# Feed-forward in-products in seven products instead of eight, accumulated over ScalarE's copies between PSUM banks

## The reference

```python
def swiglu(x, w_in, w_out):
    gate, up = jnp.split(x @ w_in, 2, axis=-1)
    return (jax.nn.silu(gate) * up) @ w_out
...
        h = h + 0.5 * swiglu(rms_norm(h, g[0]), P['ffn_w_in'][l, 0], P['ffn_w_out'][l, 0])
```

## Time and profile before

| | |
|---|---|
| Median of 3 runs | 2955.61 us (2951.46 to 2957.7) |
| Profiled execution | 2960.64 us, span 2959.0 us |
| Mean granted TensorE clock | 0.942 of full speed |
| TensorE busy | 2794.9 us, 94% |
| VectorE busy | 1185.8 us, 40% |
| ScalarE busy | 806.5 us, 27% |
| GpSimd busy | 282.6 us, 10% |
| 88 loads of in-weights | 1,024 KB each, 4.8 us to landing |

### The profile page before, as it was taken

The page is one execution under the profiler, slowest core; times in us unless marked ns, Lnnn a source line. Parts: engine busy times, 40 slices in busy tenths (PEclk is TensorE's granted clock), DMA queues, the critical chain, the costliest instruction groups (busy, mean ns, idle before and its releaser), DMA issues. The chain is left out here.

```text
span 2959.0 us, 56832 instructions
## 1 busy us (share of the span) xinstructions
PE 2794.9 (94%) x25177; PEld 2551.7 (86%) x25177; DVE 1185.8 (40%) x1738; ACT 806.5 (27%) x1261; POOL 282.6 (10%) x288
## 2 busy tenths in 40 slices
PE   7999969998999899999998989999998889999997
PEld 7999966776899746999997879999995568999997
DVE  4333355176333251433334123333444443433335
ACT  4212212132222100222221053212226762322221
POOL 1000000001111110000001200000007860000000
PEclk9999989999998557999998999999998997999998
DMA  6222210210000000322224622222222010222222
GB/s 233 82 89 86 77 64 15 71 58 30 4 3 4 33 29 26 131 82 80 95 69 120 162 100 85 85 100 85 71 74 65 23 44 29 88 90 79 99 69 75
DMA packets 36806, 214.84 MB, mean 73 GB/s; under 512 B 5232, under 2 KB 5360, under 8 KB 20880
## 3 DMA queue, kind: packets, MB, share of 16 engines
q1 hardware_dynamic: 27936, 174.34, 17.1%
q0 software_dynamic: 8720, 38.28, 4.4%
HBM read 202.49 MB, written 12.17 MB: 73 GB/s over the span
## 5 line engine op out<-in xcount | busy, mean ns | idle before, releaser
L518 PE MATMUL banks<-xh,wh 128*128 128x272 f32 x3072 | 638.7, 289 | 30.3 <-DVE wl L1484 18.0
L518 PE MATMUL banks<-xh,wl 128*128 128x272 f32 x3072 | 637.5, 289 | 0.0
L518 PE MATMUL banks<-xl,wh 128*128 128x272 f32 x3072 | 635.0, 288 | 0.0
L518 PEld LDWEIGHTS banks<-xh,wh 128*128 128x128 f32 x3072 | 485.5, 189 | 31.1 <-DVE wl L1484 23.4
L518 PEld LDWEIGHTS banks<-xl,wh 128*128 128x128 f32 x3072 | 484.7, 189 | 0.0
L518 PEld LDWEIGHTS banks<-xh,wl 128*128 128x128 f32 x3072 | 481.2, 189 | 0.0
L1484 DVE TENSOR_TENSOR wl<-raw,wh 128x2048 fp32r<-128x2048 f32 (+2 forms) x160 | 323.9, 2024 | 109.8 <-ACT wh L1133 109.7
L1133 ACT ACTIVATE wh<-raw 128x2048 fp32r<-128x2048 f32 (+2 forms) x160 | 270.7, 1692 | 260.5 <-PE banks L518 243.9
L518 PE MATMUL banks<-hh,wl 128*128 128x272 f32 x1408 | 291.4, 288 | 0.0
L518 PE MATMUL banks<-hh,wh 128*128 128x272 f32 x1408 | 291.0, 288 | 0.0
L518 PE MATMUL banks<-hl,wh 128*128 128x272 f32 x1408 | 290.2, 288 | 0.0
(11 more groups left out here) (301 smaller groups left out, 3030.6 us busy)
## 6 DMA issues: line engine op xcount, KB each, us to landing
raw<-in_w_in SPq DMA_DIRECT2D x88, 1024.0 KB, 4.8
raw<-in_w_out SPq DMA_DIRECT2D x32, 768.0 KB, 4.2
raw<-in_w_out SPq DMA_DIRECT2D x32, 640.0 KB, 3.9
raw<-in_w_rk SPq DMA_DIRECT2D x8, 1024.0 KB, 4.8
arena<-in_pages_c POOLq DMA_DIRECT2D x32, 256.0 KB, 7.6
raw<-in_w_kv SPq DMA_DIRECT2D x6, 1024.0 KB, 4.8
raw<-in_w_v SPq DMA_DIRECT2D x4, 1024.0 KB, 4.8
raw<-in_w_o SPq DMA_DIRECT2D x4, 1024.0 KB, 4.8
```

Of the source, the lines that this page charges most:

```text
L518: ins = mm(pst[:, bank + half, 0:HALF], wt[:, s, w], a[:, half * HALF:(half + 1) * HALF], start=first, stop=last)
```

## The change

An in-slot is seen as a 2 x 2 by 2 x 2 product of blocks: gate and up on one side, even and odd input tiles in the middle, the two token halves on the other side. Seven products of blocks take the place of eight (Strassen's scheme in Winograd's form). For this:

- **Weights** come in seven pieces of 512 columns: three straight from the raw slot, four sums. GpSimd makes two of them (`weight_sums`), VectorE two (in `weights`). ScalarE makes each high part, VectorE each low part, into one ring of seven pieces, which the slot in work frees piece by piece. Before, it was one instruction of 2,048 columns on each engine; now it is nine of 512 on VectorE and seven on ScalarE.
- **Activations** come in four groups j of seven operands (three blocks and four sums of 272 columns). ScalarE scales two tiles into a staging place, GpSimd makes the four sums in a chain (`operand_sums`), ScalarE the high parts (3 and then 4 operands), VectorE the low ones (`low_operands`).
- **Products** of 12 matmuls each go into one bank: 0 to x, 1 to w, 2 to x, 3 to y, 4 to x, 5 to w, 6 to z. ScalarE copies x to y after product 0, w to `sg` after 1, x to w after 2, x to z after 4 (`snap`), and TensorE accumulates on the copies. The first slot of a block (`fresh`) goes through groups as they come, and has six opening matmuls. VectorE makes up from `sg` and the banks by two additions of 272 columns, scales the gate, multiplies, and splits the hidden tile (`tail`) one slot later.
- **Stages** are 6, 6, 6 and 4 hidden tiles (`FT_IN`), so there are eight stages in a block, and there are 128 out-slots where there were 64, with 36, 36, 36 and 24 matmuls. The first two out-slots are interleaved by hidden tile.
- **GpSimd's loads** (LoRA, `g2`, `expand`, `cw1`, the table `att`) are moved behind its sums.
- Squares and root have another buffer (`rr` takes the root), and `operands_of` and `first_weights` stand at the ends of `wo`, `bo` and the out-stages.

```diff
-FTA = 12
-FTB = FT - FTA
+FT_IN = (6, 6, 6, 4)
...
+            def eighth(bank, quarter, f, b, js, start, stop):
+
+                for j in js:
+                    w = slice((4 * quarter + j) * P, (4 * quarter + j + 1) * P)
+                    xh_j, xl_j = xop_h[f][j][:, b, :], xop_l[f][j][:, b, :]
+                    for wt, x, first, last in ((ring_h, xh_j, start and j == 0, False), (ring_h, xl_j, False, False),
+                                               (ring_l, xh_j, False, stop and j == 3)):
+                        ins = mm(pst[:, bank, 0:HALF], wt[:, w], x, start=first, stop=last, skip_group_check=True)
+                return ins
...
+                else:
+                    eighth(x_bank, 0, f, 0, range(4), True, True).then_inc(eighth_done, 1)
+                    part(1)
+                    eighth(w_bank, 1, f, 5, range(4), True, True).then_inc(eighth_done, 1)
+                    part(2)
+                    snapped(1)
+                    eighth(x_bank, 2, f, 4, range(4), False, True).then_inc(eighth_done, 1)
+                    part(3)
+                    eighth(y_bank, 3, f, 1, range(4), False, True).then_inc(eighth_done, 1)
+                    part(4)
+                    snapped(3)
+                    eighth(x_bank, 4, f, 3, range(4), False, True).then_inc(eighth_done, 1)
+                pe.wait_ge(w_split[s], i + (ks + 1))
+                eighth(w_bank, 5, f, 6, range(4), False, True).then_inc(eighth_done, 1)
+                part(6)
+                snapped(4)
+                eighth(z_bank, 6, f, 2, range(4), False, True).then_inc(multiplied[s], 1)
...
+                for s in range(2):
+                    take_split(s, k0, ks)
+                    for ft in range(tiles - 2):
+                        tile(s, ft)
+                pe.wait_ge(hid_done[0], hidden + tiles // 2)
+                for s in range(2):
+                    tile(s, tiles - 2)
+                pe.wait_ge(hid_done[1], hidden + tiles // 2)
+                for s in range(2):
+                    tile(s, tiles - 1).then_inc(multiplied[s], 1)
+                with pe.Fori(1, pairs) as i:
...
```

ScalarE's order in a slot:

```diff
+                    act.wait_ge(eighth_done, 6 * k + 1)
+                    act.activation(y, x, ACT.Copy).then_inc(snap, 1)
+                    following(0)
...
+                    act.wait_ge(eighth_done, 6 * k + 2)
+                    act.activation(sg[:, s, 0:HALF], w, ACT.Copy).then_inc(snap, 1)
+                    following(1)
+                    act.wait_ge(eighth_done, 6 * k + 3)
+                    act.wait_ge(snap, 4 * k + 2)
+                    act.activation(w, x, ACT.Copy).then_inc(snap, 1)
+                    if t == 0 and n is not None:
+                        norm(n, 4)
+                    if t:
+                        tail(t - 1)
+                    following(2)
+                    act.wait_ge(eighth_done, 6 * k + 4)
+                    following(3)
+                    act.wait_ge(eighth_done, 6 * k + 5)
+                    act.activation(z, x, ACT.Copy).then_inc(snap, 1)
+                    following(4)
+                    act.wait_ge(eighth_done, 6 * k + 6)
+                    following(5)
+                    act.wait_ge(multiplied[s], k0 + t // 2 + 1)
+                    following(6)
+                    act.wait_ge(taken[s], k0 + t // 2 + 1)
+                    act.activation(sg[:, s, :], sg[:, s, :], ACT.Silu).then_inc(gate_done[s], 1)
```

VectorE's order in a slot (`following(e)` is piece e of the next slot's weights):

```diff
+                    following(0)
+                    following(1)
+                    if t:
+                        tail(t - 1)
+                    if t == 0 and before:
+                        before()
+                    following(2)
+                    following(3)
+                    dve.wait_ge(snap, 4 * k + 4)
+                    dve.tensor_tensor(up[1], x, sg[:, s, 0:HALF], ALU.add).then_inc(up_done, 1)
+                    following(4)
+                    dve.wait_ge(eighth_done, 6 * k + 6)
+                    dve.tensor_tensor(up[0], w, sg[:, s, 0:HALF], ALU.add).then_inc(up_done, 1)
+                    following(5)
...
+                    following(6)
```

GpSimd's sums, and their order in front of block 0:

```diff
+                    pool.wait_ge(landed[s], 16 * (k0 + t // 2 + 1))
+                    if n:
+                        pool.wait_ge(part_split, 6 * n - 4)
+                    pool.tensor_tensor(s3, raw_part(s, 0, 0), raw_part(s, 1, 0), ALU.subtract).then_inc(pool_sums, 1)
+                    if n:
+                        pool.wait_ge(part_split, 6 * n - 1)
+                    pool.tensor_tensor(s1, raw_part(s, 1, 0), raw_part(s, 1, 1), ALU.add).then_inc(pool_sums, 1)
...
-            for s in range(2):
-                pool.wait_ge(landed[s], 16 * 2)
+            for j in range(4):
+                operand_sums(0, j)
+            weight_sums("inA0")
```

More of the change, by code:

```diff
@@ L1133, in split, with pipeline, pair @@
                 act.activation(wh[:, s, 0:cols], raw[:, s, 0:cols], ACT.Copy).then_inc(w_hi[s], 1)
-            def pipeline(name, finish, following, first=None, unroll=False):
+            def pipeline(name, finish, following=None, after=None, begun=False, unroll=False):
                 pairs = STAGES[name][1]
[L1139 to L1142, removed]
+                def pair(i, begun=False):
+                    if not begun:
+                        split(name, i, 1)
                     finish(i, 0)
@@ L1183, in norm @@
                 act.wait_ge(sum_done, n + 1)
-                act.activation(halves(sg[:, 0, :]), bank2(bank), ACT.Sqrt, bias=eps[:, 0:1], scale=1.0 / D)\
+                act.activation(halves(rr[:]), bank2(bank), ACT.Sqrt, bias=eps[:, 0:1], scale=1.0 / D)\
                    .then_inc(root_done, 1)
-            def ffn(f, n, following=None, before=None, scaled=None):
[L1189 to L1204, removed]
@@ new lines, in ffn @@
+            def ffn(f, n, following=None, before=None, scaled=None):
+                for x, c in enumerate("ABCD"):
+                    out, k = f"out{c}{f}", end_of(f"out{c}{f}")
+                    in_stage(f"in{c}{f}", out, before if c == "A" else None)
+                    if c == "D":
+                        pipeline(out, squares(out, n, scaled), following, begun=True, unroll=scaled is not None)
+                    else:
+                        nxt = f"in{'ABCD'[x + 1]}{f}"
+                        pipeline(out, lambda i, s: None, *first_weights(nxt, k), begun=True)
@@ L1218, in _ @@
             act.wait_ge(eps_set, 3)
-            for ft in range(DT):
[L1220 to L1227, removed]
+            for j in range(4):
+                act.wait_ge(x_in[j], 16)
+                operands(0, Q_G00, j)
+                if j == 1:
+                    weights("inA0", 0, 0)
+                if j:
+                    operand_sums(0, j - 1)
+            operand_sums(0, 3)
+            for e in range(1, 7):
+                weights("inA0", 0, e)
+            for ft in range(DT):
+                square(0, ft, ft % 2)
             act.wait_ge(const_in, 16)
@@ L1574, in add @@
+            def add(name, tiles, factor, n=None, scaled=None, rooted=None, operands=None):
                 k0 = STAGES[name][0]
```

479 lines of the change are left out of this document (371 added, 108 removed).

## The result

The changed kernel takes 3,035.2 us (median of 4; 3,021.0 to 3,054.1) where the kernel before took 2,956.7 in the same series: ratio 1.0266, 95% interval 1.0223 to 1.0309. It is slower by 79 us. The forecast was 12 us more, and its range ended at 3,012. The profiled execution is the fastest of the four: 3,020.96 us, span 3,019.3, mean granted clock 0.930 (0.942 before).

What follows compares the result with a forecast made beforehand. TensorE, busy 94% of the span, was taken to bound the kernel. Terms -132.3 + 3.5 + 33 + 56 + 52 = +12 gave 2,973 profiled, forecast median 2,968 us (+0.4%), range 2,928 to 3,012.

Steps and rivals of the forecast that it cites:

- Waits and stages B to D: In-slots: 3.5 us lost to semaphore waits of seven products, plus 33 us as VectorE's loop outlasts TensorE's in later in-stages.
- Stages A: First in-stage of each block: late operands and weights delay the first scaling, 56 us lost in all (50 to 75).
- Out-stages, with `q`: Third out-slot waits for a weight buffer, stage D's cycle outlasts its matmuls, `q`'s first split is late: 52 us (44 to 60).
- the steady loop: In-slots of stages B to D: GpSimd's sums hold VectorE, so the scaling comes every 10.9 us against TensorE's 10.53.
- Rival 1: GpSimd's hold of VectorE is short, 0.8 us; TensorE sets the loop; -21 us, 2,935; chance 0.32.
- rival 2: GpSimd's hold of VectorE is long, 1.45 us; loop 11.6 us; +71 us, 3,027; chance 0.10.
- rival 3: The clock falls to 1.2 GHz in the 16 new out-stage holes; 26 us more, 2,994; chance 0.16.
- the operand sum of GpSimd at 0.65 us: Stage A: each of four chained GpSimd sums of 272 columns takes 0.65 us before the first weight pieces and copy.
- the term of block 2: Stage A, f=2: GpSimd's stores and 12 us of operand sums precede slot 0's end, near 1793.6; loss 16 us.
- Then six pieces and eight squares, 36, before the first copy: Stage A of block 0: ScalarE's operands, pieces and squares delay its first copy to 36 us; scaling at 50, loss 18.
- have tens of microseconds before use and are costed at nothing: Moved GpSimd loads (LoRA, `cw1`, table of distances): an out-stage of 24 us covers 12 us of the longest; cost nothing.
- D's cycle: Out-stage D: VectorE's cycle of 3.5 us against 3.01 of matmuls, five times; with the hole 5.5 us a layer.

## Why the prediction was wrong

The sum was to be +12 in the profiled execution; the blocks gave +85.4. Removing 132.3 is right, so 217.7 us were added, not 144.5. Two terms of the sum were too small, the stages A and the out-stages, and the fall of the clock was in neither. By stage (length less the slots' matmuls at 0.1253, and less what the kernel before loses there; how the slow matmuls divide is good to 3 us):

| Term | said | measured | of it slow matmuls |
|---|---|---|---|
| Waits and stages B to D | 36.5 | 37 | 0 |
| Stages A | 56 | 95 | 12 |
| Out-stages, with `q` | 52 | 86 | 21 |

**Right.** The mechanism of the steady loop and its size: period 10.95 (10.9), first scaling 13.9 (13.3), six slots in 66.5 us (66.4). GpSimd's sum takes 1.27 to 1.30 us undisturbed, more than the 1.18 that I took, and yet its hold in these slots is 1.0 to 1.1 as assumed: VectorE's operation began 0.2 us or more after it, so that two errors cancel, which was luck. The estimate from the Trainium skill ("GPSIMD Engine Reference", section 3.1) was 1.12; the trace has 1.27, and it decides. ScalarE's copy between banks took 0.38, not 0.43. The holes were 2.06 (1.9) in A to C and 3.24 (3.0) in D. Rival 1 fell with the duration, rival 2 with the period.

**Wrong, first: the clock (33 us).** The sum put it at nothing. It was rival 3 with 16 x 1.6 = 26 us at a chance of 0.16, set aside since "the holes are a quarter as long". I compared with the only fall that the rows showed, after 7.1 us, and took the length as evidence where the rows bounded nothing below it. In the runs a hole of 2.06 us was enough in 41 of 80 cases; of those up to 1.96 us, which the steady loop leaves, one did it. The stages A, with several waits of 2 to 13 us each, weren't in that rival at all.

**Wrong, second: stage A (27 us at full clock).** The step that failed is the operand sum of GpSimd at 0.65 us: it took 0.75 to 0.77 alone and up to 1.8 beside VectorE's low parts, which the prediction priced for weight sums and not here. The 16 sums of a block took 18.7 us in blocks 0 and 2, where 16 at 0.65 are 10.4 and the term of block 2 had 12; the chain of four in block 1 took 4.4 us, not 2.6. By block the stages A lost 32, 16, 26 and 20 us, not 18, 11, 16 and 11; in blocks 1 and 3 the first scaling came at 26.2 and 28.0 us and not at 21.8. "Then six pieces and eight squares, 36, before the first copy": the copy came at 44.4, as the pieces waited till 32.5 behind those sums, and the squares go at 0.83 each, since each waits for a sum of VectorE. Of the excess, 3 us are the opening matmuls, twelve a block and not six, and 2.4 us are only that block 0 now starts earlier (15.7, not 18.0). In the stages A, the runs on GpSimd's operand sums, its weight sums and the squares gave back some 19, 12 and 5.

**Wrong, third: out-stages at full clock (13 us).** That the moved loads "have tens of microseconds before use and are costed at nothing" asked when they are needed, and not what they delay: 8 us in block 0. And D's cycle is 3.9, not 3.5: the rows that I used, of the last slot of a block, have 0.72 us of wait for the square and none before the addition, and the loop has 0.99 and 0.15.

The profiled time rose 25 us less (60.3) than the blocks (85.4). Of these, 17.6 are the RWKV part at its other clock, 2.4 the earlier start of block 0, and the rest lies in the other unchanged parts; why the clock differs there stays open, and no run was made for it.

## What to carry to other kernels

Handing VectorE's work to GpSimd cost VectorE more than the work itself where both read two streams of SBUF: a hold of 0.8 us on average, 1.0 to 1.1 in the steady loop, against 0.61 of own work for 512 columns. So count a free engine's help by what it holds, for every sum that it takes over. When a change opens waits of 2 us and more in TensorE, price each twice, idle time and the matmuls at 1.2 GHz behind it; those up to 1.96 us here cost their length. Of a moved transfer ask which load it now meets.

## What the runs showed of the hardware

- A hole in TensorE behind some 30 matmuls at full pace brought the granted clock down to the 1.2 GHz level in 41 of 80 cases at 2.06 us, in 14 of 18 at 3.24, in 55 of 56 from 3.3 us on, in 1 of 88 from 1.7 to 1.96, and in none of 508 below 1.7 (thirteen profiles).
- A VectorE operation of 512 columns with two SBUF inputs that began beside a GpSimd sum ended 0.55 us after that sum, in 134 of 134 cases, and took up to 1.8 us in place of 0.69.
- GpSimd's addition of 512 columns with two inputs took 1.27 us alone and some 1.7 beside VectorE's; of 272 columns 0.75 alone and up to 1.8.
- ScalarE copies 272 columns from bank to bank in 0.38 us.
- Two DRAM-to-DRAM copies issued by GpSimd at the end of a stage made that slot 18.93 us long in place of 10.72.
